# Cutting an unused tail off a small scratch tensor: `early` from 13 to 5 columns, in a two-layer decoder trunk on one Trainium2 core

## The chip, the cores and the metric

The kernel is one program on one core of a Trainium2 chip. The metric is the device time of one execution in microseconds (us); less is better. A core has five engines that run on their own and meet at semaphores: TensorE (PE in the profile, with its weight loads listed as PEld), VectorE (DVE), ScalarE (ACT), GpSimd (POOL) and SyncE (SP), which here only issues transfers. SBUF is the on-chip memory of 128 partitions; "tensor X starts at byte n" means n bytes into each partition. PSUM holds what TensorE writes.

## The reference

A trunk of two layers over 512 tokens of width 1024, in float32, then a last RMSNorm.

```
for layer in range(2):
    h = rmsnorm(x, norm_mix[layer])
    if layer == 0:
        q, k, v, g, alr, u, sv = split(h @ even_w_in)
        m = concat([gla(q, k, v, g, alr), sgu(u, sv)])      # chunked linear attention; spatial gating
        x = x + m @ even_w_out
    else:
        p = h @ odd_w_in
        m = concat([rwkv7(p[:, :1696]), conformer_conv(p[:, 1696:])])   # recurrence; width-31 conv + layernorm
        x = x + m @ odd_w_out
    f = square(relu(rmsnorm(x, norm_ffn[layer]) @ w_up[layer]))          # 1024 -> 4096
    x = x + f @ w_down[layer]                                            # 4096 -> 1024
return rmsnorm(x, norm_final)
```

## The kernel before

**Matmuls.** Every large matrix product is made of three passes in the format float32r: a value is split into a high part and the rest, and `hi*hi + hi*lo + lo*hi` is summed in PSUM. Activations are kept transposed, as [128, 8, 512]. Weights come from HBM in 94 chunks of [128, 2048] (1 MB) into `w_raw`, two buffers in turn. ScalarE copies a chunk to `w_hi` (L423, L476, L606), GpSimd forms `w_lo = w_raw - w_hi` (L410), and TensorE uses `w_hi` and `w_lo` as stationary operands with `h_hi`/`h_lo` (the normed activations) or `f_hi`/`f_lo` (the squared ReLU) as moving operands of 512 columns (`tile`, L748; the first two output tiles of a down projection, L820; the first two of an up projection, L791). SP issues the load of the next chunk when `w_lo` of the chunk before in that buffer is done.

**Stages.** In order: first norm, mixer of layer 0, MLP of layer 0 (up in two halves of 2048, each followed by its half of the down projection), mixer of layer 1, MLP of layer 1, last norm. The order of the small steps in the mixers is written out by hand (`ORDER0`, `ORDER1`) and the same for all engines. Within the mixer of layer 1 VectorE runs the depthwise convolution as 31 "taps" for each of 4 channel groups: tap `j` reads `zpad[:, j:j+512]` (L1603), so that its read starts at 31 different multiples of 4 bytes.

**The scratch tensor.** `early` takes the result of a square root of one column that nobody reads. It is there to load ScalarE's square-root table ahead of its use:

```
def load_sqrt(m):
    act.activation(early[:, m:m + 1], EPS_RMS, ACT.Sqrt)      # L427
```

It is called with m = 0, 1 and 3. Columns 4 to 12 of `early` are touched by nothing.

**Where tensors lie.** The allocator of the framework lays SBUF tensors one behind another in the order in which they are made, and rounds each start up to a multiple of 32 bytes. First come the tensors that live all the time, `early` the last of them:

```
x = sb("x", [P, KD, SEQ])                     # L74; then h_hi, h_lo, w_raw, w_hi, w_lo, cols, mats, masks, low_w
eps = sb("eps", [P, 4])                       # L85
early = sb("early", [P, 13])                  # L86
```

Behind it begin, all four at the same byte, the working tensors of the stages, whose lives don't overlap: the start (`masks_f`, `x_sq`), the MLPs and norms (`f_hi`, `f_lo`, `relu`, `f_sq`, `ssq`, `xsq`, `rms`, `rrms`, `diag`, `hf`), the mixer of layer 0 (`sgu_ln` to `ln_rs`), the mixer of layer 1 (`AR` to `om_ka`). Worked out from the shapes: `x` starts at byte 16,512, `w_raw` at 65,664, `low_w` at 122,656, `eps` at 126,752 and `early` at 126,784. `early` is 13 x 4 = 52 bytes, which takes 64, so the working tensors begin at 126,848, which is 1,982 x 64.

Not all of them then start at a multiple of 64 bytes. In the mixer of layer 1 `psh` is 4,104 bytes long and takes 4,128; so `AR` to `low1` and `psh` start at a multiple of 64, and those behind it, among them `t_a` to `t_f`, `rx`, `zpad`, `cv`, `ym`, `y` and `ysq`, 32 bytes past one. `mats`, `masks` and `low_w` start 32 bytes past a multiple of 64 too.

Of the kernel before, what the change touches and what calls it, by code (L numbers as in the profile page):

```python
# [10 lines left out]
P = 128  # L11
# [48 lines left out]
def build(nc, xT_in, weights, cols_in, mats_in, masks_in, sgu_ln_in, sgu_w_in, alpha_w_in, low_w_in, out):  # L60
# [5 lines left out]
    with ctx:  # L66
        def tensors(stack):
            def sb(name, shape, dt=f32):
                return stack.enter_context(nc.sbuf_tensor(name, shape, dt))
            return sb  # L70

        sb = tensors(ctx)
# [10 lines left out]
        masks = sb("masks", [P, NMASK], u8)  # L83
        low_w = sb("low_w", [P, 2, 512])
        eps = sb("eps", [P, 4])  # L85
        early = sb("early", [P, 13])  # L86
        IDENT, ONES, BLK = mats[:, 0, :], mats[:, 1, :], mats[:, 2, :]
        EPS_RMS, EPS_LN, EPS_GN, ONE = (eps[:, i:i + 1] for i in range(4))

# [8 lines left out]
        with ExitStack() as own:  # L98
            sb = tensors(own)
# [3 lines left out]
        with ExitStack() as own:  # L103
            sb = tensors(own)
# [10 lines left out]
        with ExitStack() as own:  # L115
            sb = tensors(own)
# [30 lines left out]
        with ExitStack() as own:  # L147
            sb = tensors(own)
# [1598 lines left out]
```

## Time and profile before

| | |
|---|---|
| median of 3 runs | 1428.9 us (1428.59 to 1431.68) |
| profiled execution | 1428.9 us, span from first to last instruction 1427.1 us |
| TensorE busy (matmul) | 1297.5 us, 91% of the span, 8452 instructions |
| VectorE, GpSimd, ScalarE busy | 687.7, 449.6, 420.6 us |
| mean granted TensorE clock | 0.956 of full speed |
| DMA | 106.17 MB, 74 GB/s over the span |

The profile's times are of one execution. A busy TensorE is not one at its peak, since a matmul's row lasts longer than the step to the next one: what counts is the distance between starts.

### The profile page before, as it was taken

How to read it: one execution, taken by the hardware profiler on the slowest of the kernel's cores; microseconds unless marked ns; L12 is line 12 of the kernel's file. 1: busy time of each engine (PE TensorE's matmuls, PEld its weight loads, DVE VectorE, ACT ScalarE, POOL GpSimd, SP SyncE). 2: the span in 40 equal slices, each digit the busy share in tenths (PEclk: the TensorE clock that was granted, in tenths of full speed). 3: DMA queues.
4: the chain of work that ended last, by engine and by line, in shares of the span. 5: the costliest groups of instructions: out<-in, count | busy, mean ns of one | idle time of the engine just before them, and what ended most of it. 6: DMA issues, size and time to landing. Idle time of an engine off the chain costs nothing. (4 is left out here: it accounts for less than half of the span.)

```text
span 1427.1 us, 20378 instructions
## 1 busy us (share of the span) xinstructions
PE 1297.5 (91%) x8452; PEld 1046.7 (73%) x8452; DVE 687.7 (48%) x972; ACT 420.6 (29%) x535; POOL 449.6 (32%) x101
## 2 busy tenths in 40 slices
PE   4999897999999999898798898777879999999997
PEld 3898876888888888676666566564668888888886
DVE  6216355552004421386868878686665420144213
ACT  3537222322112311262435233222322221122110
POOL 3332323344444454321121110110224444344441
PEclk9999998999999999999999987898989999999998
DMA  5321222123223222301001010000021322232221
GB/s 193 112 89 60 63 86 89 59 92 114 89 88 103 103 89 90 115 30 60 31 31 60 20 41 2 30 32 1 30 89 59 113 93 89 100 105 88 89 89 59
DMA packets 16802, 106.17 MB, mean 74 GB/s; under 512 B 1872, under 2 KB 2144, under 8 KB 4704
## 3 DMA queue, kind: packets, MB, share of 16 engines
q1 hardware_dynamic: 15872, 103.83, 21.3%
q10 hardware_dynamic: 864, 1.36, 0.3%
q8 instruction: 53, 0.87, 0.3%
q14 instruction: 13, 0.11, 0.0%
HBM read 103.09 MB, written 2.10 MB: 74 GB/s over the span
## 5 line engine op out<-in xcount | busy, mean ns | idle before, releaser
L410 POOL TENSOR_TENSOR w_lo<-w_raw,w_hi 128x2048 fp32r<-128x2048 f32 x94 | 444.8, 4732 | 940.3 <-ACT w_hi L476 352.3
L748 PE MATMUL ps<-h_hi,w_hi 128*128 128x512 f32 x792 | 323.7, 409 | 8.6 <-DVE h_lo L1199 4.9
L748 PE MATMUL ps<-h_hi,w_lo 128*128 128x512 f32 x792 | 312.9, 395 | 0.0
L748 PE MATMUL ps<-h_lo,w_hi 128*128 128x512 f32 x792 | 312.6, 395 | 0.0
L748 PEld LDWEIGHTS ps<-h_hi,w_hi 128*128 128x128 f32 x792 | 151.1, 191 | 58.7 <-issue 19.5
L476 ACT ACTIVATE w_hi<-w_raw 128x2048 fp32r<-128x2048 f32 x58 | 111.1, 1915 | 266.8 <-PE ps L748 197.1
L748 PEld LDWEIGHTS ps<-h_hi,w_lo 128*128 128x128 f32 x792 | 151.1, 191 | 32.5
L748 PEld LDWEIGHTS ps<-h_lo,w_hi 128*128 128x128 f32 x792 | 151.4, 191 | 31.1 <-issue 2.2
L1253 DVE TENSOR_TENSOR x<-x,ps 128x512 f32 (+1 forms) x32 | 22.0, 688 | 294.9 <-PE ps L748 226.0
L1236 DVE TENSOR_TENSOR f_hi<-relu 128x512 f32 x64 | 71.7, 1120 | 172.2 <-ACT relu L462 160.2
L748 PE MATMUL ps<-f_hi,w_hi 128*128 128x512 f32 x384 | 149.4, 389 | 0.0
L748 PE MATMUL ps<-f_lo,w_hi 128*128 128x512 f32 x384 | 149.4, 389 | 0.0
L748 PE MATMUL ps<-f_hi,w_lo 128*128 128x512 f32 x384 | 149.4, 389 | 0.0
L1603 DVE SCALAR_TENSOR_TENSOR cv<-zpad,cols,cv 128x512 f32<-128x512 f32 x120 | 103.2, 860 | 3.2
L462 ACT ACTIVATE relu<-ps 128x512 f32<-128x512 f32 x56 | 33.5, 599 | 222.2 <-PE ps L748 222.2
L748 PEld LDWEIGHTS ps<-f_hi,w_hi 128*128 128x128 f32 x384 | 72.1, 188 | 15.1
L748 PEld LDWEIGHTS ps<-f_lo,w_hi 128*128 128x128 f32 x384 | 72.1, 188 | 14.9
L748 PEld LDWEIGHTS ps<-f_hi,w_lo 128*128 128x128 f32 x384 | 72.1, 188 | 14.9
L863 PE MATMUL ps<-w_hi,h_hi 128*128 128x256 f32 x256 | 75.8, 296 | 3.7 <-ACT u_tok L526 3.7
L423 ACT ACTIVATE w_hi<-w_raw 128x2048 fp32r<-128x2048 f32 x25 | 47.8, 1911 | 88.5 <-PE ps L748 70.4
L863 PE MATMUL ps<-w_lo,h_hi 128*128 128x256 f32 x256 | 73.8, 288 | 0.0
L863 PE MATMUL ps<-w_hi,h_lo 128*128 128x256 f32 x256 | 73.8, 288 | 0.0
(279 smaller groups left out, 1768.7 us busy)
## 6 DMA issues: line engine op xcount, KB each, us to landing
w_raw<-in_weights SPq DMA_DIRECT2D x94, 1024.0 KB, 4.9
outT<-x SPq DMA_DIRECT2D x8, 256.0 KB, 2.2
x<-in_xT ACTq DMA_DIRECT2D x4, 256.0 KB, 5.7
x<-in_xT SPq DMA_DIRECT2D x4, 256.0 KB, 5.1
masks_f<-in_masks SPq DMA_DIRECT2D x1, 768.0 KB, 13.1
low_w<-in_low_w SPq DMA_DIRECT2D x1, 512.0 KB, 13.8
sgu_ln<-in_sgu_ln SPq DMA_DIRECT2D x1, 512.0 KB, 3.6
sgu_w<-in_sgu_w SPq DMA_DIRECT2D x1, 256.0 KB, 3.8
```

Of the source, the lines that this page charges most:

```text
L410: pool.tensor_tensor(w_lo[:, j, :], w_raw[:, j, :], w_hi[:, j, :].bitcast(f32), SUB)\
L423: act.activation(w_hi[:, n % 2, :], w_raw[:, n % 2, :], ACT.Copy).then_inc(s("hi_done"), 1)
L462: act.activation(relu[:, g % 2, :], bank(g % 2), ACT.Relu).then_inc(s("relu_done"), 1)
L476: act.activation(w_hi[:, n % 2, :], w_raw[:, n % 2, :], ACT.Copy).then_inc(s("hi_done"), 1)
L748: mm = pe.matmul(bank(gb(g) if isinstance(i, int) else g % 2), w, r, start=(k == 0 and m == 0), stop=(k == K - 1 and m == 2))
L863: mm = pe.matmul(bank(g % 2, 0, 256), a, b, start=(k == 0 and m == 0), stop=(k == KD - 1 and m == 2))
L1236: tt(f_hi[:, bass.ds(4 * i + c, 1), :].rearrange("p a n -> p (a n)"), relu[:, g % 2, :], relu[:, g % 2, :], MUL).then_inc(s("fhi_done"), 1)
L1253: tt(xk, xk, bank(g % 2), ADD).then_inc(s(f"gemm_evac{g % 2}"), 1)
L1603: stt(cv[:, c, :], zpad[:, j:j + SEQ], col("conv_w", TAPS * c + j), cv[:, c, :], MUL, ADD)\
```

## The change

One line: `early` gets 5 columns in place of 13.

```
         eps = sb("eps", [P, 4])
-        early = sb("early", [P, 13])
+        early = sb("early", [P, 5])
```

Five columns are 20 bytes, which takes 32 by the allocator's rounding, where 52 took 64. No instruction is added, removed or reordered, and no shape that an instruction works on changes. `x`, `h_hi`, `h_lo`, `w_raw`, `w_hi`, `w_lo`, `cols`, `mats`, `masks`, `low_w`, `eps` and `early` stay where they are. Every working tensor behind `early` starts 32 bytes lower: the first at 126,816. Those that started at a multiple of 64 bytes now start 32 bytes past one, and the other way round.

## Rows read from the trace of the kernel before

**Rows 1.** Span, stages (us, PE, PEld, DVE, ACT, POOL busy), granted clock.

```profile
core 0: 1427.1 us, clock 0.956
0.00:50.00 50.00, 27.75 (x122) 22.02 (x123) 27.84 (x58) 23.57 (x31) 18.65 (x10) 0.93 0.53 196
50.00:248.00 198.00, 182.16 (x1302) 163.21 (x1301) 87.45 (x152) 79.34 (x99) 64.34 (x14) 0.97 0.23 75
248.00:610.00 362.00, 354.84 (x1562) 293.44 (x1561) 118.26 (x150) 84.11 (x73) 153.26 (x32) 0.99 0.27 93
610.00:1017.00 407.00, 340.14 (x3743) 243.36 (x3742) 309.11 (x430) 143.91 (x254) 50.84 (x11) 0.92 0.09 30
1017.00:1065.00 48.00, 40.17 (x177) 33.15 (x176) 30.07 (x37) 11.95 (x11) 18.33 (x4) 0.88 0.26 88
1065.00:1427.10 362.10, 352.39 (x1554) 291.53 (x1553) 114.97 (x150) 77.74 (x67) 144.20 (x30) 0.98 0.25 87
```

**Rows 2.** The chain that ended last, in order of time (start, length, what).

```profile
1086.60 65.57 PE ps L748 x288
1152.17 21.76 PE ps L820 x96
1173.93 152.32 PE ps L748 x672
```

**Rows 3.** By line: `early` (ns min/median/max) and `f` matmuls (us busy, mean ns).

```profile
L427 ACT ACTIVATE early<-eps x3: 203/203/204, 5.1 to 1043.4; 128x1 f32<-128x1 f32 x3
L748 PE MATMUL ps<-f_hi,w_hi 128*128 128x512 f32 x384 | 149.4, 389 | 0.0
L820 PE MATMUL ps<-f_hi,w_hi 128*128 128x512 f32 x128 | 49.8, 389 | 0.0
```

**Rows 4.** Timeline of TensorE: first down projection, then half clock.

```profile
539.97 0.39 PE L748 MATMUL ps<-f_hi,w_lo 128*128 128x512 f32 x1
540.20 0.39 PE L748 MATMUL ps<-f_hi,w_hi 128*128 128x512 f32 x1
540.43 0.39 PE L748 MATMUL ps<-f_lo,w_hi 128*128 128x512 f32 x1
...
541.33 0.39 PE L748 MATMUL ps<-f_hi,w_lo 128*128 128x512 f32 x1
...
606.34 0.63 PE L748 MATMUL ps<-h_lo,w_hi 128*128 128x512 f32 x1
...
609.32 0.63 PE L748 MATMUL ps<-h_hi,w_lo 128*128 128x512 f32 x1
```

**Rows 5.** Float32 matmuls by line (ns min/median/max), moving operands at both phases.

```profile
L1132 PE MATMUL ps<-y,mats x8: 592/644/697, 757.3 to 995.7; 128*128 128x512 f32 x8
L1135 PE MATMUL ps<-ysq,mats x8: 592/644/697, 771.5 to 999.8; 128*128 128x512 f32 x8
L1139 PE MATMUL ps<-low,low_w x8: 590/644/1223, 794.8 to 1002.7; 96*128 96x512 f32 x8
```

**Rows 6.** VectorE and ScalarE by line (ns min/median/max), operands at both phases.

```profile
L1603 DVE SCALAR_TENSOR_TENSOR cv<-zpad,cols,cv x120: 707/752/5042, 669.5 to 976.6; 128x512 f32<-128x512 f32 x120
L1367 DVE TENSOR_TENSOR sv<-sv,sgu_ln x4: 691/692/693, 106.3 to 123.5; 128x512 f32<-128x512 f32 x4
L1586 DVE TENSOR_TENSOR y<-y,ysq x4: 691/692/693, 783.3 to 1004.5; 128x512 f32<-128x512 f32 x4
L462 ACT ACTIVATE relu<-ps x56: 598/599/600, 273.8 to 1326.3; 128x512 f32<-128x512 f32 x56
L589 ACT ACTIVATE psh<-ps x14: 572/599/602, 617.5 to 901.4; 128x512 f32<-128x512 f32 x14
```

**Rows 7.** GpSimd by line, and the DMA issues by size and landing.

```profile
L410 POOL TENSOR_TENSOR w_lo<-w_raw,w_hi x94: 4495/4662/5010, 13.8 to 1393.6; 128x2048 fp32r<-128x2048 f32 x94
L405 POOL TENSOR_TENSOR x_sq<-x_sq x3: 1264/1647/1661, 6.7 to 12.0; 128x512 f32<-128x512 f32 x3
w_raw<-in_weights SPq DMA_DIRECT2D x94, 1024.0 KB, 4.9
masks_f<-in_masks SPq DMA_DIRECT2D x1, 768.0 KB, 13.1
low_w<-in_low_w SPq DMA_DIRECT2D x1, 512.0 KB, 13.8
```

**Rows 8.** The norm before the second MLP: VectorE by line, GpSimd's timeline, the chain.

```profile
L1190 DVE TENSOR_SCALAR diag<-mats,rrms x20: 273/279/3558, 18.6 to 1417.2; 128x128 f32<-128x128 f32 x20
1053.06 4.50 POOL L410 TENSOR_TENSOR w_lo<-w_raw,w_hi 128x2048 fp32r<-128x2048 f32 x1 [6.25 <-ACT w_hi L423]
1054.08 3.57 DVE diag L1190
```

**Rows 9.** Timelines of VectorE and GpSimd around the longest tap of the mixer.

```profile
810.41 8.97 DVE L1603 SCALAR_TENSOR_TENSOR cv<-zpad,cols,cv 128x512 f32<-128x512 f32 x6
812.71 4.54 POOL L410 TENSOR_TENSOR w_lo<-w_raw,w_hi 128x2048 fp32r<-128x2048 f32 x1 [37.33 <-ACT w_hi L606]
```

## The prediction

> **What bounds the kernel now.** I read the table of stages first [rows 1]. The two MLP stages, 362.0 and 362.1 us, have a matmul running for 354.8 and 352.4 us: there TensorE alone sets the time. The mixer of layer 1 is the other long stage, 407 us with 340 us of matmul and 309 us of VectorE, so small dependent steps count there as well. The chain that ended last then shows what the MLP's time consists of [rows 2]: three unbroken pieces of matmuls, 288, 96 and 672 of them, from 1086.60 to 1326.25 us, with nothing between them. 1,056 matmuls in 239.65 us are 0.227 us each. The timeline shows the same step [rows 4]: six steps from 539.97 to 541.33 us, 0.2267 us from start to start, though each row lasts 0.39. So time is gained or lost in an MLP only by what changes that step, and in the mixers by what changes a step on a chain between engines.
>
> **The change part by part.** The edit adds and removes no instruction. What can cost or pay is of two kinds: the instructions that touch `early`, and the 32 bytes by which the working tensors move.
>
> *Those on `early`.* There are three [rows 3], 0.203 us each, one column wide, into columns 0, 1 and 3, which both shapes have and whose addresses stay. Cost 0. They keep their table load with them too, so nothing is late afterwards.
>
> *Streams that don't move.* `w_raw`, `w_hi`, `w_lo`, `x`, `h_hi`, `h_lo` and the constants keep their bytes. With that the 94 loads of 1 MB, all 94 of GpSimd's 4.7 us differences [rows 7] and all matmuls on `h_hi`/`h_lo` read and write where they did. Cost 0, and no range from it.
>
> *Transfers that move.* Only `masks_f`, `sgu_ln`, `sgu_w` and `alpha_w` land behind `early`, once each. The nearest pair: `masks_f` (768 KB, at a multiple of 64 bytes) took 13.1 us and `low_w` (512 KB, 32 past one, queued right behind it) 13.8 [rows 7]. These two overlap, so they price no phase; they say that a landing is of that size and that there are four. I take 0. GpSimd's three sums of `x_sq` (1.6 us at most, rows 7) move as well, ahead of 20 us; 10% of them would be 0.5 us.
>
> *VectorE and ScalarE on moved tensors.* The trace has both phases side by side. A product of two SBUF operands at a multiple of 64 bytes, `sv`, is 691/692/693 ns; one 32 bytes past it, `y`, is 691/692/693 ns [rows 6]. The taps are a better test still: their read begins at 30 offsets of 4 bytes each, so through every phase of a 64-byte line, and yet the median of 120 is 752 ns, with 707 the least. ScalarE writes `relu` at a multiple of 64 bytes in 599 ns and `psh`, 4 bytes past the start of its row, in a median of 599. So phase costs neither engine anything that these rows resolve, and they resolve 1 ns in 692: of VectorE's 688 us that is 1 us, were all of it on the path. I take 0.
>
> *Float32 matmuls on moved tensors.* `y` and `ysq` start 32 bytes past a multiple of 64, `low1` at one. Such matmuls of 512 columns, two instructions each, take 592 to 697 ns for `y` and `ysq`, median 644; for `low1` the shortest is 590 and the median the same 644 [rows 5]. (Its 1223 is at half clock.) A difference of at most 2 ns, which the 96 rows of `low1` against 128 may make by themselves. I take 0 for all small matmuls of the mixers.
>
> *Float32r matmuls on `f_hi` and `f_lo`.* This is the one stream that the trace shows at one phase only. There are 3 x (384 + 128) = 1,536 of them, all with the moving operand in `f_hi` or `f_lo` [rows 3], and the two other forms of each line have the same counts, and at the chain's 0.2267 us they are 348 us of the span. Both bounds come from the step. At half clock seven steps from 606.34 to 609.32 us are 0.4257 us each [rows 4]; half of that is 0.2129, so at full clock a matmul carries 13.8 ns which don't scale with the clock, of unknown cause. If these belonged to how the operand lies, the move could at best take them away, 1,536 x 13.8 ns = 21.2 us, or, as the size of one more such stall, add as much. The nearest row for the phase is the float32 pair of [rows 5], 0 to 2 ns; it is nearer than the step because it compares phases and the step doesn't. I take 0. `h_hi` and `h_lo` lie at the same phase as `f` before the edit, and the chain's third piece, which mixes both, has the same step [rows 2], so the trace has no float32r counter-example.
>
> The Trainium skill, in "TensorE: Matmul & The Clock Gate", section "Wait — 56ns, not 53.3ns?", gives back-to-back starts at full clock as the columns at 2.4 GHz plus about 2.5 ns, 215.7 ns for 512 columns. This case's 226.7 ns is 11 ns more. By the page's figure as the reachable step the moved stream could be 1,536 x 11 = 17 us shorter, an estimate from that page; nothing in it ties the excess to addresses.
>
> *The sum.* 0 + 0 + 0 + 0 + 0 + 0. The profiled execution took 1428.9 us, 1.8 us more than its span, and is itself the median of the runs shown. So the forecast is 1428.9 us, no change. The runs spread from 1428.59 to 1431.68, 0.2% of the time; about 0.2%, 2.9 us either way, is what a measurement of this kernel can tell from no change.
>
> **The rivals.**
>
> *The float32r stream is slower 32 bytes past a multiple of 64.* It decides from 1.9 ns per matmul on (2.9 us over 1,536). With the whole stall of 13.8 ns the time is 1428.9 + 21.2 = 1450.1 us, with half of it 1439.5. For it: it is the one unproved stream, TensorE is saturated just there, and a float32r row of 512 columns is 389 ns long [rows 3] where the shortest float32 one is 592 [rows 5], so float32r takes its columns in faster than the pair that was compared. Against it: the float32 pair shows nothing at all, and neither do two other engines. Chance 0.08.
>
> *The float32r stream is faster there.* The same mechanism with the other sign: 1428.9 - 21.2 = 1407.7 us at best. No row speaks for it but the unexplained 13.8 ns. Chance 0.02.
>
> *A collision between VectorE and GpSimd appears or goes away.* Some VectorE instructions stretch while GpSimd runs `w_lo`. The first `diag` of the norm before the second MLP began 1.02 us into a `w_lo` of 4.50 us and took 3.56 us where the median is 0.279, and it stands on the chain with 3.57 us [rows 8]. The longest tap, 5.04 us against 0.752 [rows 6], is one of six that took 8.97 us together around the `w_lo` of 812.71 us [rows 9]. So one collision more or less is worth 3.3 us at a norm and up to 4.3 at a tap: 1425.6 or 1424.6 us with one less on the path, 1432.2 or 1433.2 with one more. In the norm, one engine would have to be a microsecond early or late; the edit changes no duration, which speaks against it, while the spread of 3.1 us between unchanged runs is of that size, which speaks for it as an accident. Chance 0.10, half to each side.
>
> That collision is what the Trainium skill, "SBUF — State Buffer", section "Who interferes with whom", calls an exclusive lock on a shared pair of ports, where whoever comes second waits for the whole instruction. The trace agrees for `diag`, which ends (1054.08 + 3.57) 0.09 us after the `w_lo` (1053.06 + 4.50). Nothing in that rule depends on an address, so it adds no way for the edit to act.
>
> *The edit does nothing at all.* Were starts rounded to 64 bytes rather than 32, 20 and 52 bytes would take the same room and both programs would be one. The time would be 1428.9 us again; it can't be told from the forecast by the clock. It is part of the forecast's chance.
>
> **How the numbers follow.** No change, 0.80. Faster by over 0.2%: 0.02 for the stream and 0.05 for a lost collision, 0.07. Slower: 0.08 and 0.05, 0.13. The forecast's own range is 1426.0 to 1431.8 us. The cases of a collision reach to 1425.0 and 1433.5 us with a little for the run's own spread; that range takes in 0.90 and leaves out the stream's two cases. The unknown cost of the stream, from -21.2 to +21.2 us, is larger, but holding it takes a width that the remaining 0.1 doesn't ask for.
>
> **What the profile after would show.** Right: six steps in the down projection still take 1.36 us; `f` matmuls still at 389 ns in all 1,536; products at 692 ns, now with the phases exchanged; taps at 752; the MLP stages 362 us to within 1; span near 1427. Wrong, and how: steps of 0.229 us or more in the down projection (lines 748 and 820 with `f`) while those with `h` stay at 0.227, which is the stream's phase; or every step the same but a `diag`, an `xsq` or a tap of over 3 us in a new place, which is a collision; or a shift in when the granted clock is at its half level, with no instruction changed, which none of my steps has and which would make the forecast wrong for a reason outside the edit.

## The result: 10.9 us slower, and the profile after

| | before | after |
|---|---|---|
| median of 4 runs each | 1428.77 us (1428.59 to 1431.68) | 1439.67 us (1438.53 to 1441.72) |
| ratio after / before, 95% interval | | 1.0072 [1.0055, 1.0088] |
| profiled execution, span | 1428.9 us, 1427.1 us | 1437.61 us, 1435.8 us |
| granted clock, mean | 0.956 | 0.958 |

The forecast was no change, 1425.0 to 1433.5 us. The time lies outside it, on the slower side. In what follows a **step** is the time from the start of a matmul to the start of the next, and the **three-pass sum** is the sum of the steps of the passes hi\*w_hi, lo\*w_hi and hi\*w_lo, averaged over a down projection at full clock. Where nothing else is said, steps are means over the starts in the trace, since a single start is shown only to 10 ns; the means were taken from the recorded starts, which are whole ns.

The stages of the kernel after, in the columns of [rows 1], cut at nearly the same points of the work (the first cut is at 50.00 us in both, where the kernel after was already 2.6 us further on):

```profile
core 0: 1435.8 us, clock 0.958
0.00:50.00 50.00, 29.04 (x144) 24.70 (x145) 30.58 (x61) 25.68 (x34) 18.61 (x10) 0.97 0.53 196
50.00:246.00 196.00, 180.17 (x1282) 161.13 (x1282) 86.13 (x150) 77.46 (x98) 64.27 (x14) 0.97 0.23 76
246.00:613.00 367.00, 359.84 (x1561) 293.46 (x1560) 118.11 (x150) 84.19 (x74) 153.23 (x32) 0.98 0.27 92
613.00:1021.00 408.00, 340.94 (x3741) 242.73 (x3740) 308.49 (x428) 143.39 (x254) 50.88 (x11) 0.92 0.09 30
1021.00:1069.00 48.00, 40.17 (x178) 33.10 (x177) 30.00 (x37) 11.93 (x11) 18.30 (x4) 0.88 0.26 88
1069.00:1435.80 366.80, 357.10 (x1555) 291.26 (x1553) 115.11 (x150) 77.70 (x67) 144.13 (x30) 0.98 0.25 86
```

The two MLP stages hold the same number of matmuls as in [rows 1], to one, and take 367.0 and 366.8 us in place of 362.0 and 362.1. In them VectorE, ScalarE and GpSimd are busy for the same time as before, to 0.2 us. The chain that ended last says which part of an MLP grew. Its five pieces of matmuls in the second MLP, after:

```profile
1090.75 65.57 PE ps L748 x288
1156.32 22.40 PE ps L820 x96
1178.72 154.26 PE ps L748 x672
1332.99 22.40 PE ps L820 x96
1355.39 67.22 PE ps L748 x288
```

The last two of before, which [rows 2] leaves out:

```profile
1326.25 21.76 PE ps L820 x96
1348.01 65.29 PE ps L748 x288
```

The first piece is all up projection, with `h` as the moving operand: 65.57 us both times. The pieces of line 820 are all `f`: 21.76 became 22.40 us, 0.64 us over 96 matmuls, 6.7 ns each. The last piece is all `f`: +1.93 us over 288, again 6.7 ns. The long piece of 672 grew by 1.94 us, not by 672 x 6.7 ns = 4.5: it has 288 matmuls on `f` and 384 on `h`, and only the 288 pay. Together 5.15 us in this MLP, 2.57 in each half. The lines of the moving operand `f_lo`, duration as least, median and most, before:

```profile
L748 PE MATMUL ps<-f_lo,w_hi x384: 389/389/389, 355.5 to 1412.7; 128*128 128x512 f32 x192
L820 PE MATMUL ps<-f_lo,w_hi x128: 389/389/389, 333.7 to 1347.4; 128*128 128x512 f32 x128
```

and after, with `h_lo` of the same line below them:

```profile
L748 PE MATMUL ps<-f_lo,w_hi x384: 395/396/396, 353.5 to 1422.0; 128*128 128x512 f32 x192
L820 PE MATMUL ps<-f_lo,w_hi x128: 395/396/397, 331.1 to 1354.8; 128*128 128x512 f32 x128
L748 PE MATMUL ps<-h_lo,w_hi x792: 387/389/632, 25.0 to 1332.4; 128*128 128x512 f32 x198
```

Every one of the `f` matmuls is longer, and `h` is not: the least and the most of the 384 differ by 1 ns. That speaks against a collision with another engine, since GpSimd is busy for only 153 of the 367 us of the stage and ScalarE for 84. Sorted by what GpSimd does when a matmul of `f` starts, the step is 233.3 ns for the 636 that start during a `w_lo` and 233.4 ns for the 900 that don't. TensorE's timeline gives the step that [rows 4] gave as 0.2267 us, now at the same place of the first down projection:

```profile
540.62 0.40 PE L748 MATMUL ps<-f_lo,w_hi 128*128 128x512 f32 x1
...
542.02 0.40 PE L748 MATMUL ps<-f_lo,w_hi 128*128 128x512 f32 x1
```

Six steps are 1.40 us, 0.2333 each. Over 1,536 matmuls 6.67 ns make 10.2 us; the interval of the ratio says 7.9 to 12.6 us. So that one number accounts for the loss.

The two profiled executions differ by only 8.7 us of span, and this too can be followed. The start of the first `f_lo` matmul of line 820 came 2.6 us earlier than before (331.1 against 333.7), a gain from the first 60 us that another run need not have. The four down halves give 4 x 2.57 = 10.3. In the mixer of layer 1 a further 1.6 us was lost between 608 and 977 us; about half of that is the granted clock, at its half level for 13 full `h` matmuls at the start of the mixer where [rows 4] has 9 (605.77 to 609.32 us), at 0.43 against 0.23 us each. The last norm was 0.6 us shorter, its small matmuls (L755, L772) 1.07 and 1.73 us in place of 1.30 and 2.09, because the granted clock fell to its half level within L772 (at 1426.46 us) where before it had fallen within L755 (at 1415.46 us). -2.6 + 10.3 + 1.6 - 0.6 = 8.7.

The other moved instructions, after:

```profile
L427 ACT ACTIVATE early<-eps x3: 203/203/203, 5.1 to 1047.6; 128x1 f32<-128x1 f32 x3
L1132 PE MATMUL ps<-y,mats x8: 592/644/697, 761.2 to 999.8; 128*128 128x512 f32 x8
L1139 PE MATMUL ps<-low,low_w x8: 590/644/1223, 798.8 to 1006.8; 96*128 96x512 f32 x8
L1603 DVE SCALAR_TENSOR_TENSOR cv<-zpad,cols,cv x120: 722/752/5052, 673.4 to 980.7; 128x512 f32<-128x512 f32 x120
L1367 DVE TENSOR_TENSOR sv<-sv,sgu_ln x4: 691/692/693, 103.7 to 120.8; 128x512 f32<-128x512 f32 x4
L1586 DVE TENSOR_TENSOR y<-y,ysq x4: 691/692/693, 787.2 to 1008.6; 128x512 f32<-128x512 f32 x4
L462 ACT ACTIVATE relu<-ps x56: 598/598/600, 271.2 to 1333.0; 128x512 f32<-128x512 f32 x56
L589 ACT ACTIVATE psh<-ps x14: 571/598/600, 620.8 to 905.5; 128x512 f32<-128x512 f32 x14
```

Against [rows 3, 5, 6] they are the same to 1 ns in the median, with their phases exchanged. The three instructions on `early`, two other engines and the float32 matmuls don't see the move. The 644 ns of a float32 matmul is the mean of its two rows, 697 and 592; the steps behind them are 533 and 523 ns both times.

### The profile page after: what moved, and what is told of

It is laid out like the page before. It is cut to its first block and busy times, and to the rows that moved or that the text cites. A ratio compares the mean times of both kernels' runs of the same rounds, so it can differ in the third digit from the quotient of the medians.

```text
span 1435.8 us, 20378 instructions
## 1 busy us (share of the span) xinstructions
PE 1307.3 (91%) x8452; PEld 1046.4 (73%) x8452; DVE 688.4 (48%) x972; ACT 420.4 (29%) x535; POOL 449.4 (31%) x101
## 5 line engine op out<-in xcount | busy, mean ns | idle before, releaser
L410 POOL TENSOR_TENSOR w_lo<-w_raw,w_hi 128x2048 fp32r<-128x2048 f32 x94 | 444.7, 4731 | 949.9 <-ACT w_hi L476 362.0
```

Source lines behind the costliest of these rows:

```text
L410: pool.tensor_tensor(w_lo[:, j, :], w_raw[:, j, :], w_hi[:, j, :].bitcast(f32), SUB)\
```

## The experiments

In the records below, theory A is the prediction's first rival as it stood: a moving operand in float32r is slow when it starts 32 bytes past a multiple of 64. Theory F, formed after the first batch, says that no address by itself matters, but the place of the moving operand relative to the weights, counted within some hundred bytes. Its two forms date from after the second batch. F1 has the weights meant that are being loaded while the operand streams (those of the next pass), F2 the weights that the pass itself multiplies with. Before the change `f_hi`, `f_lo` and `w_hi`, `w_lo` are a multiple of 256 bytes apart (0 below); after it `f` is at -32.

### First batch: whose move is it, and is it the phase?

`e1_up32` moves the working tensors 32 bytes up in place of down, `e2_up64` 64 bytes up.

```diff
-        early = sb("early", [P, 13])
+        early = sb("early", [P, 21])   # e1; [P, 29] in e2
```

> early gets 21 columns: 84 bytes take 96, so that every working tensor lies 32 bytes higher than before instead of 32 lower, again 32 bytes past a multiple of 64. Theory A (the phase of f_hi and f_lo against 64 bytes sets the matmul step): as the changed kernel, 1428.9 + about 10.5 = 1439.4 us, and the f matmuls have rows of 396 ns. Theory B (only the lower place costs, by a neighbour or an absolute address): 1428.9 us and 389 ns. Theory C (the cost is an accident of the order in which engines meet): any value from 1425 to 1433 us, with 389 ns.

> early gets 29 columns: 116 bytes take 128, so that every working tensor lies 64 bytes higher than before. Theory A with lines of 64 bytes: 1428.9 us, f matmuls at 389 ns. Were it lines of 128 bytes or more, f would now be 64 bytes past a multiple of 128 and the time some 1439 us with 396 ns or above. Theory B (any move costs): 1439 us.

`e3_f_alone` leaves `early` at 13 columns and moves `f_hi` and `f_lo` alone, by a pad of 32 bytes ahead and one behind, so that the rest of the MLP's tensors are 64 bytes up and the mixers' where they were. `e4_f_back` is the changed kernel with `f_hi` and `f_lo` put back, and with them all tensors of the MLPs and norms, which lie behind them; those of the start and of the mixers stay moved.

```diff
+            pad_a = sb("pad_a", [P, 8])
             f_hi = sb("f_hi", [P, HALF_K, SEQ], f32r)
             f_lo = sb("f_lo", [P, HALF_K, SEQ], f32r)
+            pad_b = sb("pad_b", [P, 8])    # e3 alone
```

> Only the f tensors get the new phase: early stays at 13 columns, a pad of 32 bytes goes ahead of f_hi and another behind f_lo, so that f_hi and f_lo lie 32 bytes past a multiple of 64 and all behind them 64 bytes higher, at the old phase. Both mixers stay as before. Theory A: the whole loss, 1439.4 us, 396 ns. Theory D (the mixers' tensors carry part of the loss): less than 10.5 us of it, about 8 by the drift of 1.7 us that the two profiles show in the mixer of layer 1.

> The changed kernel (early with 5 columns) with a pad of 32 bytes ahead of f_hi: the tensors of the MLPs and norms are back where they were, the mixers' tensors stay 32 bytes lower. Theory A: 1428.9 us, 389 ns. Theory D: what the mixers carry stays, some 1430.6 us.

Measured, on one chip. The kernel before had a median of 1430.07 us there, 22 of its 23 runs from 1422.58 to 1432.76 (one more was of 7050 us).

| | median us | ratio to before | three-pass sum, `f` |
|---|---|---|---|
| e1_up32 | 1439.11 | 1.0060 [1.0048, 1.0073] | 700.0 ns |
| e2_up64 | 1432.40 | 1.0019 [1.0006, 1.0032] | 686.8 ns |
| e3_f_alone | 1438.33 | 1.0059 [1.0046, 1.0072] | 700.0 ns |
| e4_f_back | 1428.14 | 0.9986 [0.9973, 0.9998] | 680.0 ns |

The lines of `f` in e3_f_alone, and then in e4_f_back:

```profile
L750 PE MATMUL ps<-f_lo,w_hi x384: 393/395/397, 353.6 to 1415.7; 128*128 128x512 f32 x192
```

```profile
L749 PE MATMUL ps<-f_lo,w_hi x384: 389/389/389, 354.1 to 1414.6; 128*128 128x512 f32 x192
```

With the mixers untouched the step of 700.0 ns for three passes is there (e3), and the loss of 8.3 us (6.6 to 10.3) agrees with it. With the start and the mixers moved and the MLPs' tensors put back it is gone (e4), so the place of the former costs nothing. The other tensors of the MLPs went with `f` in e4, but in e3 they kept their place against a multiple of 64 bytes and the sum was 700.0 all the same. The direction doesn't matter (e1). But e2 doesn't fit theory A: 64 bytes up the start is a multiple of 64 again, and still the three passes take 686.8 ns, each another time:

```profile
L748 PE MATMUL ps<-f_hi,w_hi x384: 394/394/394, 359.3 to 1420.9; 128*128 128x512 f32 x192
L748 PE MATMUL ps<-f_lo,w_hi x384: 388/388/388, 359.6 to 1421.2; 128*128 128x512 f32 x192
L748 PE MATMUL ps<-f_hi,w_lo x384: 392/392/398, 359.8 to 1421.4; 128*128 128x512 f32 x192
```

The steps are 231.7, 225.8 and 229.3 ns. The phase against 64 bytes is not the whole rule.

### Second batch: which places, and against what?

`e5_scan32` puts each of the 16 slices of `f` (one slice of 512 columns is a moving operand) 32 bytes further than the one before, `e6_scan4` 4 bytes further (there a pad of 448 bytes ahead of `f_lo` gives its slices the same places as those of `f_hi`). `e7_w32_scan32` is e5 with `w_hi` and `w_lo` moved up by 32 bytes, and what lies behind them moved by 512. `e8_h32` moves `h_hi` and `h_lo` alone.

```diff
-            f_hi = sb("f_hi", [P, HALF_K, SEQ], f32r)
+            f_hi = sb("f_hi", [P, HALF_K, SEQ + 8], f32r)   # f_lo the same; SEQ + 1 in e6
-  ... f_hi[:, k, :], f_lo[:, k, :]
+  ... f_hi[:, k, 0:SEQ], f_lo[:, k, 0:SEQ]
```

```diff
+        pad_a = sb("pad_a", [P, 8])
         h_hi = sb("h_hi", [P, KD, SEQ], f32r)     # e8; ahead of w_hi, and behind w_lo, in e7
         h_lo = sb("h_lo", [P, KD, SEQ], f32r)
+        pad_b = sb("pad_b", [P, 120])
```

> f_hi and f_lo get a pitch of 520 columns (2,080 bytes) in place of 512, so that slice k of the sixteen starts 32 x k bytes further round a circle of 512 bytes: one down projection then shows the step of the matmul at sixteen places, 32 bytes apart. Theory A with a plain 64-byte line: slices k even have rows of 389 ns and a step of 226.7 ns, k odd 396 ns and 233.3 ns, all even ones alike and all odd ones alike; time 1428.9 + 5 = 1434 us. Theory E (moved 64 bytes the step was already 228.9 on the mean, so the pattern is wider than 64 bytes): only k = 0 and those a larger power of two away keep 226.7 ns, and the even ones differ among themselves. Either way a place with less than 226.7 ns would make a faster kernel.

> f_hi and f_lo get a pitch of 513 columns, so that slice k starts 4 x k bytes past the old place: sixteen places inside 64 bytes. Theory A: k = 0 at 226.7 ns, all others at about 233.3 ns. If the cost grows by a unit of 16 or 32 bytes the steps come in groups of 4 or 8 slices. Time 1428.9 to 1439 us.

> As the scan in steps of 32 bytes, and w_hi and w_lo, the stationary operands, lie 32 bytes higher. Theory F (the step depends on how the moving operand lies against the weights that are loaded beside it): the pattern over k turns by one place against the scan with w in its old place. Theory A (the moving operand alone): the pattern over k stays. The tokens' matmuls, where w is the moving operand of 256 columns and h the stationary one, go from 120 to 126.7 ns by theory A.

> Only h_hi and h_lo lie 32 bytes higher, 32 past a multiple of 64; all else keeps its place round 512 bytes. Theory A: the 2,376 matmuls at line 748 with h, and the 192 beside them, step by 233.3 ns at full clock: 2,500 x 6.67 ns = 16.7 us, less what the mixer of layer 1 hides, so 1440 to 1446 us, and f stays at 226.7. At half clock 426.7 ns as before, if the cost is of the memory and not of TensorE's own clock. Theory G (f is special, by its loops or its writer): 1428.9 us.

Measured on one chip, before 1430.39 us there. e5, e6 and e7 are one run each: 1436.37, 1430.89 and 1454.47 us. The finding is in the three-pass sums of slice 0 to 15 (ns):

```
e5, +32 each: 692 694 699 701 700 703 694 694 | 694 692 701 701 700 703 694 695
e7, the same: 695 693 694 699 701 700 704 694 | 694 694 693 701 701 700 704 694
e6, +4 each:  685 707 700 705 700 703 692 684 | 699 713 689 690 691 701 701 687
```

e5 repeats after 8 slices, 256 bytes, and its slowest stretch is slices 2 to 5. In e7, with the weights 32 bytes up and `f` where e5 has it, the same sequence stands one slice later, at 3 to 6: the pattern went with the weights. The 1454.47 us of e7 have a plain reason: with the weights moved `h` is displaced too, and its three-pass sum is 699.8 ns. Slice 0 of e5, at the place of before, takes 692 ns and not 680, so a step also depends on its neighbours. In e6 the sum jumps by up to 24 ns from one slice to the next, and the first four slices, within 16 bytes, have 685, 707, 700 and 705: steps as small as 4 bytes count.

e8_h32: 1439.01 us (1434.58 to 1441.08), ratio 1.0059 [1.0035, 1.0083]. Its lines of `f` and of `h`:

```profile
L750 PE MATMUL ps<-f_lo,w_hi x384: 389/389/389, 359.9 to 1424.9; 128*128 128x512 f32 x192
L750 PE MATMUL ps<-h_lo,w_hi x792: 390/396/628, 25.1 to 1337.8; 128*128 128x512 f32 x198
```

Now `h` steps are 233.1 to 233.5 ns and `f` stays at 226.7. Its 3 x 856 matmuls by 6.7 ns would be 17 us were all of them at full clock with TensorE the bound; measured were 8.4 us (5 to 12), less than I had expected. The maximum of 628 ns, a row at the half level of the clock, is no longer than the 632 of the kernel after, and the mean step of `h` there is 426.7 ns in both kernels, before and e8: at that level the place costs nothing. The trace shows where the loss falls in the profiled execution. The up half between two down halves, 384 matmuls on `h`, takes 89.83 us in place of 87.27, which is 2.56 us or 384 x 6.67 ns. From the last `f` matmul of the first MLP to the first of the second it takes 560.2 us in place of 557.6; that is one up half, so the mixer of layer 1 lost nothing on balance, although some 720 of the `h` matmuls stand in it.

### Third batch: relative or absolute, and which weights?

`e9_all_up32` moves every tensor of the program 32 bytes up, so that each start changes its phase and no distance does. `e10_wlo32` moves `w_lo` alone.

```diff
+        pad_a = sb("pad_a", [P, 8])
         x = sb("x", [P, KD, SEQ])                    # e9
```

```diff
+        pad_a = sb("pad_a", [P, 8])
         w_lo = sb("w_lo", [P, 2, 2048], f32r)        # e10
+        pad_b = sb("pad_b", [P, 120])
```

> A pad of 32 bytes ahead of x, early back at 13 columns: every tensor of the kernel lies 32 bytes higher, h, w and f alike, all 32 past a multiple of 64, and none has moved against another. Theory A (the start against 64 bytes): all 1,536 f matmuls and some 2,500 h matmuls step by 233.3 ns, so 1450 us or above. Theory F (how moving operand and weights lie against each other): 226.7 ns everywhere and 1428.9 us.

> Only w_lo lies 32 bytes higher; w_hi, h and f keep their places round 512 bytes. The passes run hi*w_hi, lo*w_hi, hi*w_lo. Theory F1 (a stream collides with the load of the NEXT weights, which runs beside it): the pass lo*w_hi, beside which w_lo is loaded, goes to 233 ns, the two others stay near 226.7. Theory F2 (it collides with its own weights' place): the pass hi*w_lo goes to 233 ns. Theory A: none changes. By F1 or F2 a third of all 512-column matmuls pays 6.7 ns: 1428.9 + some 8 = 1437 us.

Before had 1428.52 us on that chip. e9_all_up32: 1429.72 us, ratio 1.0008 [0.9992, 1.0024]. Its lines of `f` and of `h`:

```profile
L749 PE MATMUL ps<-f_lo,w_hi x384: 389/389/389, 352.7 to 1410.0; 128*128 128x512 f32 x192
L749 PE MATMUL ps<-h_lo,w_hi x792: 387/389/628, 24.9 to 1322.9; 128*128 128x512 f32 x198
```

All is as before the change, with `f`, `h` and `w` all at the phase that theory A calls slow. Theory A is refuted, and what counts is relative.

e10_wlo32: 1451.81 us (1448.51 to 1453.89), ratio 1.0167 [1.0136, 1.0199], the slowest with an interval. Its lines of `f`:

```profile
L750 PE MATMUL ps<-f_hi,w_hi x384: 395/395/395, 358.3 to 1434.0; 128*128 128x512 f32 x192
L750 PE MATMUL ps<-f_lo,w_hi x384: 400/400/400, 358.5 to 1434.2; 128*128 128x512 f32 x192
L750 PE MATMUL ps<-f_hi,w_lo x384: 389/389/389, 358.8 to 1434.5; 128*128 128x512 f32 x192
```

The steps are 232.6, 239.4 and 228.0 ns: +6.0, +12.7 and +1.3. The pass that multiplies with the moved `w_lo` hardly changed. The one ahead of it, lo\*w_hi, in which neither operand moved but during which `w_lo` is being loaded, changed most. The timeline shows that load (named by the pass that it is for) beside the pass ahead:

```profile
545.41 0.40 PE L750 MATMUL ps<-f_lo,w_hi 128*128 128x512 f32 x1
545.42 0.19 PEld L750 LDWEIGHTS ps<-f_hi,w_lo 128*128 128x128 f32 x1
545.65 0.39 PE L750 MATMUL ps<-f_hi,w_lo 128*128 128x512 f32 x1
```

That refutes F2. It speaks for F1, not cleanly: hi\*w_hi rose too, and beside it `w_hi` is loaded, which didn't move. The three steps together are 700.0 ns, the same sum as when `f` moves against both weights. The expected time of some 1437 us, a third of the matmuls paying, missed by 15 us: all three passes share the 20 ns, and `h` pays as `f` does (three-pass sum 699.0 ns, 682.0 before), 4,104 matmuls in all, where the change of this document touches 1,536.

### The map of places

Four kernels give `f` another place in each of the four down halves, so that each has 384 matmuls at one place: `e11_sweep_a`, `e12_sweep_b` and `e14_sweep_c` move `f_hi` and `f_lo` together, `e13_flo_alone` leaves `f_hi` where it was and moves `f_lo`.

```diff
+            f_hi_all = sb("f_hi", [P, HALF_K * SEQ + 128], f32r)   # f_lo_all the same
+        F_AT = [24, 32, 40, 48]       # columns of 4 bytes: e11
+                                      # e12 [1, 4, 12, 60]; e14 [2, 20, 28, 63]
+                                      # e13 [8, 16, 32, 4], for f_lo alone
```

> f_hi and f_lo start at four places, one for each half of each MLP, in this order: 96, 128, 160 and 192 bytes past the old place (0 is 226.7 ns, 32 on either side 233.3, 64 is 228.9 on the mean). Theory F with a circle of 256 bytes: 192 as its mirror 64 (228.9), 96 and 160 alike (some 233), 128 unknown: 226.7 if the circle is 128 bytes, else up to 233. If some place lies under 226.7 the bound of 213.3 ns is open and a faster kernel follows. Time 1428.9 to 1439 us.

> As the sweep before with 4, 16, 48 and 240 bytes past the old place. Theory F with a unit of 16 bytes: 4 keeps about 226.7 (the same 16-byte unit in 3 of 4 columns) or rises a little, 16, 48 and 240 at some 230 to 233 ns. With a unit of 32 bytes 4 and 16 keep 226.7 and 48 and 240 pay. Time 1428.9 to 1439 us.

> f_hi stays at its old place, f_lo alone starts 32, 64, 128 and 16 bytes past its own, for the four halves of the MLPs in order. Theory F1 (a stream collides with the weights loaded beside it): only the pass lo*w_hi streams f_lo, so it alone goes up, and the other two stay at 226.7 ns, unless a stall in one pass also shifts the next. If the two others rise as much, the neighbours' rhythm matters as much as the pass's own place. Time up to 1436 us.

> f_hi and f_lo together start 8, 80, 112 and 252 bytes past the old place. So far every place tried costs more than the old one (64: 686.8 ns for three passes, 16: 695, 32, 48, 96, 128, 192 and 240: 700, 160: 703, 4: 714, against 680). Theory F expects 8 and 252 (4 back) above 700 ns and none under 680. A place under 680 would make a kernel faster than both.

One run each, e11 to e14: 1439.28, 1443.09, 1432.31 and 1431.89 us. Runs of the unchanged kernel lie up to 11 us apart (1421.36 to 1432.48 on the chip of e11 and e12; on that of e13 and e14 it has one run, 1429.06), so the trace's steps are the measurement. The granted clock is part of that spread: e14 had 0.964 on the mean and e12 0.950. All places together, three-pass sum against the distance of `f` from its old place (after is -32, the same as 224 modulo 256):

| bytes | ns | bytes | ns | bytes | ns |
|---|---|---|---|---|---|
| 0 (before, e4, e9) | 680.0 | 48 | 700.0 | 160 | 702.8 |
| 4 | 713.9 | 64 (e2) | 686.8 | 192 | 700.0 |
| 8 | 697.5 | 80 | 693.3 | 224 (after) | 700.0 |
| 16 | 695.0 | 96 | 700.1 | 240 | 700.0 |
| 32 (e1, e3) | 700.0 | 112 | 693.2 | 252 | 692.5 |
| | | 128 | 699.9 | | |

For the place +4 of e12_sweep_b and the place +160 of e11_sweep_a, the groups of one down half (busy us, mean ns):

```profile
L754 PE MATMUL ps<-f_hi,w_hi 128*128 128x512 f32 x96 | 38.5, 401 | 0.0
```

```profile
L754 PE MATMUL ps<-f_hi,w_hi 128*128 128x512 f32 x95 | 37.7, 397 | 0.0
```

With `f_lo` alone moved (e13) the sums are 695.0 (+32), 695.9 (+64), 686.7 (+128) and 696.1 (+16). At +128 only the pass that streams `f_lo` grew, steps of 226.7, 234.3 and 225.7 ns:

```profile
L755 PE MATMUL ps<-f_lo,w_hi 128*128 128x512 f32 x95 | 37.5, 395 | 0.0
L755 PE MATMUL ps<-f_hi,w_hi 128*128 128x512 f32 x96 | 37.3, 389 | 0.0
L755 PE MATMUL ps<-f_hi,w_lo 128*128 128x512 f32 x95 | 36.9, 388 | 0.0
```

At the other three all passes grew (at +32: 232.0, 233.0 and 230.0), though two of them stream an operand that didn't move. My expectations missed in several places: +192 as the mirror of +64 (700.0 against 686.8), +4 near the old place (713.9, the slowest of all), and for e14 over 700 ns at +8 and +252 because +4 was so slow (697.5 and 692.5). The map has no slope that a formula of mine gives. What it shows for certain is that of 16 places the old one is the best, by 6.8 ns over the next, and that none has a shorter three-pass sum (single passes do go lower, 225.0 ns at +112); so no version that beats the kernel before came out of this.

## Why the prediction was wrong, step by step

**The step that failed** is a term of the sum: "*Float32r matmuls on `f_hi` and `f_lo`* ... I take 0." It is +6.67 ns for each of the 1,536, 10.2 us. The count was right and the bound held. Its size was read from times shown to 10 ns: over the 57 such steps at the half clock of the trace before the mean is 426.67 ns, so the excess at full clock is 13.3 ns and not 13.8, 20.5 us over the stream and not 21.2. The first rival's case "with half of it 1439.5" met the median of 1439.67 us; its chance was 0.08. That the half was met is luck, since nothing in the prediction spoke for a half, and at other distances the same stream pays between 2.3 and 11.3 ns. What went wrong is the choice between the ends. I took 0 because the float32 pair compares phases, and the experiments show that this pair could not speak for float32r: moved by the same 32 bytes, `y`, `ysq` and `low1` stayed at 644 ns while each matmul on `f` took 6.7 ns more. I had noted in the rival's favour that the float32 row is 592 ns or more where the float32r row is 389, so that the pair takes its columns more slowly, and I gave it too little weight. Whether that is why float32 is spared is not shown.

**The rival was right in place, near in size by luck, and wrong in mechanism.** "The float32r stream is slower 32 bytes past a multiple of 64": e9 has it there at full speed, e2 has it slower at a multiple of 64. What decides is where the moving operand lies against the weights. The step "`w_raw`, `w_hi`, `w_lo`, `x`, `h_hi`, `h_lo` keep their bytes ... cost 0" was right for this change, but its thought was not safe: e10 moved `w_lo` alone and made the passes slower whose operands kept their bytes. Likewise the sentence that `h` at the same phase gives no counter-example looked at the phase alone; that `f`, `h` and `w` all lay at one place modulo 256 bytes was the thing worth seeing.

**The rest held.** The three instructions on `early` 203 ns, VectorE's products 692 ns at exchanged phases, taps 752, ScalarE 598, float32 matmuls 644 [rows 3, 5, 6]; that the moves of the start and the mixers cost nothing is shown by e4, 0.9986 [0.9973, 0.9998], which has every move but those in the MLPs and norms. No further collision of the kind of [rows 8, 9] is needed for the 10.9 us. The observable that the prediction named, steps of 0.229 us or more with `f` while those with `h` stay at 0.227, is what came: 0.2333 and 0.2267.

**What stays open.** e10 shows that the place of the weights being loaded for the next pass matters, and e10 and e13 that slowness spills into neighbouring passes; which accesses meet, and why +64 costs a third of what +32 does, and +4 most of all, is not settled. The 13.3 ns that the step at the old place has over half of its length at half clock are unexplained too. A test of passes in another order, or with one set of weights for many matmuls, would be the next; neither was run.

The Trainium skill, "SBUF — State Buffer", section "Who interferes with whom", says that TensorE never waits on anyone, and its section "A bandwidth-pool intuition that's wrong (but worth ruling out)" gives the weight loads a second, independent read port. No run here shows a matmul slowed by another engine's reads or writes; but e10, where moving `w_lo` by 32 bytes lengthened the pass during which it is loaded by 12.7 ns, does not agree that its two reads are independent. The Trainium skill, "Advanced Engine Details and Errata", section "SBUF Cachelines", has lines of 16 bytes; taken alone, it gives no reason for +16 and +32 bytes to cost anything, and they measured 695.0 and 700.0 ns against 680.0.

## What to carry to other kernels

When a stream saturates its engine and the trace shows it at one placement only, the rows of a slower format are weak evidence for it, as they were here; give the stream's own unexplained excess a real chance. And read the step between starts for each group of a line, since the chain of one profile, pieces of 96, 288 and 672 matmuls, was enough to say which operand had slowed.

## What was unexpected of the hardware

- The step of a float32r matmul of 512 columns at full clock depends on the distance between the moving operand and the weights. The pattern repeats after 256 bytes in the one scan that shows it (e5). The step is 226.7 ns at 0, 233.3 at 32 either way, 238.0 on average at 4 (713.9 / 3). The address itself didn't matter in the one shift that was tried (e9: 226.7 with everything 32 bytes up).
- A move of the weights that are loaded beside a pass can cost that pass more (+12.7 ns, lo\*w_hi in e10) than the pass that uses them (+1.3).
- Not every distance from 0 is bad for every form: the 256-column matmuls of the first layer's mixer, in which `w` is the moving operand and `h` the weights, took 119.8 ns from start to start before, 116.9 with `w` moved up by 32 bytes (e7) and 118.3 with `h` moved (e8).
- VectorE, ScalarE and float32 matmuls of 644 ns showed nothing of the kind, and float32r steps at the half level of the clock neither (426.7 ns with `h` moved in e8 and in the kernel before).
